# Attention with scores from one-pass halves of two heads at a time, and value products that carry the row sums

## The reference

```python
q = rmsnorm(q.reshape(B, N, 8, 64), g_q)          # 8 query heads
k = rmsnorm(k.reshape(B, N, 2, 64), g_k)          # 2 key heads, 4 query heads each
...
k_all = jnp.concatenate([kc_, kl], axis=1)        # 256 context + 512 latent keys
v_all = jnp.concatenate([vc_, vl], axis=1)
...
def gqa_attend(qb, k, v):
    s = jnp.einsum('bqhgd,bkhd->bhgqk', qb, k, preferred_element_type=jnp.float32) * HEAD_DIM ** -0.5
    p = jax.nn.softmax(s, axis=-1)
    return jnp.einsum('bhgqk,bkhd->bqhgd', p.astype(v.dtype), v)
```

## Time and profile before

| | |
|---|---|
| runs | 4133.22, 4141.39, 4142.72 us; median 4141.39 |
| the profiled execution | 4152.68 us; its span from first to last instruction 4149.8 us |
| busy share of the span | PE 87%, PEld 73%, DVE 55%, ACT 30%, POOL 28% |
| mean granted TensorE clock | 0.916 of full speed |
| attention, layer 0 | 451.95 us (first copy of keys) to 628.0 us (last unit_out) |
| attention, layer 1 | 1667.64 us to 1797.1 us |

### The profile page before, as it was taken

How to read it: one execution, slowest core, us unless ns; L and a number is a source line. 1 busy time by engine, 2 the same in 40 slices (tenths; PEclk the granted TensorE clock), 3 DMA queues, 4 the chain that set the end, 5 groups by cost and what they waited for, 6 DMA issues and landing times. The chain is left out here.

```text
span 4149.8 us, 56879 instructions
## 1 busy us (share of the span) xinstructions
PE 3610.2 (87%) x22004; PEld 3014.9 (73%) x22004; DVE 2273.7 (55%) x3284; ACT 1255.5 (30%) x1878; POOL 1162.5 (28%) x564
## 2 busy tenths in 40 slices
PE   5976797899998976889996999798999996987998
PEld 3766576788887765667885788677777775765886
DVE  4669462655546448535445588733666655326334
ACT  4123222211222123223323354432333432323222
POOL 5214002222222203024441333143222220423442
PEclk8988599899999988999998999899999997998998
DMA  4420001223222430013331211121011110212221
GB/s 164 154 93 1 0 1 61 77 97 112 97 91 93 142 105 1 1 58 115 117 111 44 77 66 71 36 102 67 32 47 37 41 47 1 102 61 72 98 95 60
DMA packets 85332, 295.30 MB, mean 71 GB/s; under 512 B 13506, under 2 KB 14082, under 8 KB 84740
## 3 DMA queue, kind: packets, MB, share of 16 engines
q1 hardware_dynamic: 84836, 290.74, 19.8%
q10 hardware_dynamic: 288, 1.60, 0.1%
HBM read 290.21 MB, written 2.10 MB: 70 GB/s over the span
## 5 line engine op out<-in xcount | busy, mean ns | idle before, releaser
L221 POOL TENSOR_TENSOR mlp_slab_lo<-slab,mlp_slab_hi 128x1024 fp32r<-128x1024 f32 x192 | 477.1, 2488 | 889.2 <-ACT mlp_slab_hi L204 889.2
L119 PE MATMUL banks<-mlp_hid_hi,mlp_slab_hi 128*128 128x512 f32 (+1 forms) x1024 | 375.0, 366 | 8.9 <-DVE mlp_hid_lo L1798 8.9
L120 PE MATMUL banks<-mlp_hid_lo,mlp_slab_hi 128*128 128x512 f32 (+1 forms) x1024 | 372.7, 364 | 0.0
L121 PE MATMUL banks<-mlp_hid_hi,mlp_slab_lo 128*128 128x512 f32 (+1 forms) x1024 | 372.4, 364 | 0.0
L204 ACT ACTIVATE mlp_slab_hi<-slab 128x1024 fp32r<-128x1024 f32 x192 | 202.4, 1058 | 528.8 <-PE banks L121 400.9
L119 PE MATMUL banks<-hT_mlp_hi,mlp_slab_hi 128*128 128x512 f32 (+1 forms) x768 | 276.6, 360 | 15.5 <-issue 8.7
L1798 DVE TENSOR_TENSOR mlp_hid_lo<-mlp_sq,mlp_hid_hi 128x512 fp32r<-128x512 f32 (+1 forms) x96 | 216.4, 2254 | 117.9 <-ACT mlp_hid_hi L1756 117.5
L120 PE MATMUL banks<-hT_mlp_lo,mlp_slab_hi 128*128 128x512 f32 (+1 forms) x768 | 275.7, 359 | 0.0
L121 PE MATMUL banks<-hT_mlp_hi,mlp_slab_lo 128*128 128x512 f32 (+1 forms) x768 | 274.9, 358 | 0.0
L119 PEld LDWEIGHTS banks<-mlp_hid_hi,mlp_slab_hi 128*128 128x128 f32 x1024 | 194.2, 190 | 43.8 <-DVE mlp_hid_lo L1798 13.8
L121 PEld LDWEIGHTS banks<-mlp_hid_hi,mlp_slab_lo 128*128 128x128 f32 x1024 | 194.0, 189 | 30.3
(11 more groups left out here) (532 smaller groups left out, 9330.4 us busy)
## 6 DMA issues: line engine op xcount, KB each, us to landing
slab<-in_s_mlp_dram SPq DMA_DIRECT2D x192, 512.0 KB, 3.5
proj_vec_slab<-in_s_vec_proj_dram SPq DMA_DIRECT2D x64, 512.0 KB, 3.7
mlp_vec_slab<-in_s_vec_mlp_dram SPq DMA_DIRECT2D x64, 512.0 KB, 3.5
slab<-in_s_ssm_dram SPq DMA_DIRECT2D x48, 512.0 KB, 3.5
slab<-in_s_gdn_dram SPq DMA_DIRECT2D x48, 512.0 KB, 3.5
slab<-in_s_in_dram SPq DMA_DIRECT2D x32, 512.0 KB, 4.6
slab<-in_s_out_dram SPq DMA_DIRECT2D x24, 512.0 KB, 4.2
slab<-in_s_merge_ssm_dram SPq DMA_DIRECT2D x24, 512.0 KB, 3.5
```

The source lines that it names most:

```text
L119: nc.tensor.matmul(out, lhs.hi, rhs.hi, start=start, stop=False)
L120: nc.tensor.matmul(out, lhs.hi, rhs.lo, start=False, stop=False)
L121: return nc.tensor.matmul(out, lhs.lo, rhs.hi, start=False, stop=stop)
L221: self.nc.gpsimd.tensor_tensor(pair.lo[:], self.raw[u % slots][:], pair.hi[:].bitcast(F32), ALU.subtract).then_inc(self.split, 1)
```

## The change

Only `attention` changes.

1. Queries and keys are split when they are prepared: ScalarE rounds each transposed tile to `hi` (queries times 1/8 already), VectorE writes `lo` (a difference). Query tiles that no unit needs (the context tiles in layer 1) are no longer prepared.
2. Scores are made for two heads at a time (units 2m and 2m+1), as three float32r products each; the matmuls of the even head use rows 0 to 63 of the array and banks 0 and 1, those of the odd head rows 64 to 127 and banks 2 and 3, in alternation. Scores of pair m wait for both exponentials of pair m-1.
3. Values are copied to `vs` with a column of ones behind each key head, so that a product has 2 x 65 = 130 columns and the row sum comes out of it. The reciprocal is taken from PSUM, in `unit_out`.
4. The row maximum is negated in the same instruction. The exponential has no scale and no accumulation.
5. ScalarE copies the first four transposed blocks, VectorE the other two.

```diff
+    prep = [(t, "keys") for t in range(C)] + [(t, "heads") for t in range(first, C)]
-        qkT = sb("qkT", [P, 6, TOK])
+        qs = sbuf_pair(st.held.enter_context, nc, f"{name}_qs", [P, HEADS_Q // 2, (C - first) * P])
+        ks = sbuf_pair(st.held.enter_context, nc, f"{name}_ks", [P, HEADS_KV, TOK])
+        vs = sb("vs", [P, C, HEADS_KV, HD + 1])
...
             def _(act):
+                for n, (t, what) in enumerate(prep):
+                    src, pair = prepared(n)
+                    act.wait_ge(turned, n + 2)
+                    nc.scalar.activation(pair.hi, src, ACT.Copy, scale=1.0 if what == "keys" else HD ** -0.5).then_inc(rounded, 1)
+                def exp(n):
+                    act.wait_ge(maxed, n + 2)
                     if n >= 2:
                         act.wait_ge(p_turned, n)
+                    nc.scalar.activation(p_[:, n % 2, 0:keys(units[n][1]) * P], scored_in(n), ACT.Exp, bias=sm[:, 0, n:n + 1]).then_inc(exped, 1)
+                def turned_out(n):
+                    act.wait_ge(p_turned, n + 2)
+                    if n >= 2:
+                        act.wait_ge(o_full, n)
+                    w = min(keys(units[n][1]), 4) * P
+                    nc.scalar.activation(pT[:, n % 2, 0:w], c.ps[:, 4 + 2 * (n % 2), 0:w], ACT.Copy).then_inc(pT_first, 1)
+                exp(0)
+                exp(1)
+                for n, (h, t) in enumerate(units):
+                    if n % 2 == 0:
+                        turned_out(n)
+                    if n + 2 < len(units):
+                        exp(n + 2)
+                    if n % 2:
+                        turned_out(n)
...
             def _(dve):
+                nc.vector.memset(vs[:, :, :, HD:], 1.0)
+                nc.vector.tensor_copy(vs[:, :, :, 0:HD], c.tok[:, :, C_AV:C_AV + P].rearrange("p t (g e) -> p t g e", g=HEADS_KV)).then_inc(v_ready, 1)
+                for n, (t, what) in enumerate(prep):
+                    src, pair = prepared(n)
+                    dve.wait_ge(rounded, n + 2)
+                    nc.vector.scalar_tensor_tensor(out=pair.lo, in0=src, scalar=1.0 if what == "keys" else HD ** -0.5,
+                                                   in1=pair.hi.bitcast(F32), op0=ALU.mult, op1=ALU.subtract).then_inc(split, 1)
+                def row_max(n):
+                    dve.wait_ge(scored, n // 2 + 2)
+                    nc.vector.tensor_reduce(sm[:, 0, n:n + 1], scored_in(n), AX, ALU.max, negate=True).then_inc(maxed, 1)
+                def unit_out(n):
+                    h, t = units[n]
+                    col = 256 + (HD + 1) * (h // 4)
+                    dve.wait_ge(o_full, n + 2)
+                    nc.vector.reciprocal(sm[:, 1, n:n + 1], c.ps[:, 5 + 2 * (n % 2), col + HD:col + HD + 1]).then_inc(inverted, 1)
+                    dve.wait_ge(inverted, n + 2)
+                    nc.vector.tensor_scalar(c.tok[:, t, C_AQ + h * HD:C_AQ + (h + 1) * HD], c.ps[:, 5 + 2 * (n % 2), col:col + HD],
+                                            sm[:, 1, n:n + 1], None, ALU.mult).then_inc(o_read, 1)
+                def turned_rest(n):
...
+                for n in range(0, len(units), 2):
+                    if n + 2 < len(units):
+                        row_max(n + 2)
+                        row_max(n + 3)
+                    turned_rest(n)
+                    if n:
+                        unit_out(n - 1)
+                    turned_rest(n + 1)
+                    unit_out(n)
...
             def _(pe):
+                def scores(m):
+                    h, t = units[2 * m]
+                    if m:
+                        pe.wait_ge(exped, 2 * m + 1)
+                    q = qs[:, h // 2, (t - first) * P:(t - first + 1) * P]
+                    k = ks[:, h // 4, :]
+                    spans = ((0, HALF), (HALF, TOK)) if keys(t) == TILES else ((0, CTX),)
+                    for b, (s0, s1) in enumerate(spans):
+                        for e, (x, y) in enumerate(((q.hi, k.hi), (q.lo, k.hi), (q.hi, k.lo))):
+                            for n in range(2):
+                                r = slice(64 * n, 64 * n + 64)
+                                last = nc.tensor.matmul(c.ps[:, 2 * n + b, 0:s1 - s0], x[r], y[r, s0:s1], start=e == 0, stop=e == 2)
+                    last.then_inc(scored, 1)
                 def weighted(n):
+                    pe.wait_ge(pT_first, n + 2)
+                    if keys(t) > 4:
+                        pe.wait_ge(pT_rest, wide_before(n) + 2)
                     for s in range(keys(t)):
+                        last = nc.tensor.matmul(c.ps[:, 5 + 2 * (n % 2), 256:256 + HEADS_KV * (HD + 1)], pT[:, n % 2, s * P:(s + 1) * P],
+                                                vs[:, s, :, :].rearrange("p g e -> p (g e)"), start=s == 0, stop=s == keys(t) - 1)
...
                 for n, (h, t) in enumerate(units):
-                    if n + 1 < len(units):
-                        scores(n + 1)
+                    if n % 2 == 0 and n + 2 < len(units):
+                        scores(n // 2 + 1)
                     pe.wait_ge(exped, n + 2)
                     if n >= 2:
                         pe.wait_ge(o_read, n)
```

More of the change, by code:

```diff
@@ L1361, in _ @@
-                unit_out(dve, len(units) - 1)
+                last.then_inc(k_ready, 1)
+                nc.vector.memset(vs[:, :, :, HD:], 1.0)
[5 more added lines that the diff above has]
+                                                   in1=pair.hi.bitcast(F32), op0=ALU.mult, op1=ALU.subtract).then_inc(split, 1)
@@ new lines, in turned_rest @@
+                def turned_rest(n):
+                    nk = keys(units[n][1])
+                    if nk > 4:
+                        dve.wait_ge(p_turned, n + 2)
+                        if n >= 2:
+                            dve.wait_ge(o_full, n)
+                        nc.vector.tensor_copy(pT[:, n % 2, HALF:nk * P], c.ps[:, 5 + 2 * (n % 2), 0:nk * P - HALF]).then_inc(pT_rest, 1)
+                row_max(0)
+                row_max(1)
+                for n in range(0, len(units), 2):
[7 more added lines that the diff above has]
+                    unit_out(n)
@@ L1363, in _ @@
+                unit_out(len(units) - 1)
             @block.tensor
             def _(pe):
-                pe.wait_ge(qk_ready, 2)
-                n = 0
-                for t in range(C):
-                    src = [c.tok[:, t, C_AQ + P * j:C_AQ + P * j + P] for j in range(4)] + \
-                          [kdup[:, t, 2 * j:2 * j + 2, :].rearrange("p d e -> p (d e)") for j in range(2)]
-                    for half in range(2):
-                        if n >= 8:
-                            pe.wait_ge(placed, n - 6)
-                        for j in range(3):
-                            last = nc.tensor.transpose(c.ps[:, n % 8, j * P:(j + 1) * P], src[3 * half + j], c.ident)
-                        last.then_inc(turned, 1)
-                        n += 1
@@ L1377, in _ @@
-                pe.wait_ge(placed, 2 * C + 1)
-                def scores(n):
-                    h, t = units[n]
-                    r = slice(64 * (h % 2), 64 * (h % 2) + 64)
-                    if n >= 2:
-                        pe.wait_ge(exped, n)
-                    q = qkT[r, h // 2, t * P:(t + 1) * P]
-                    for b, (s0, s1) in enumerate(((0, HALF), (HALF, TOK)) if keys(t) == TILES else ((0, CTX),)):
-                        last = nc.tensor.matmul(c.ps[:, 2 * (n % 2) + b, 0:s1 - s0], q, qkT[r, 4 + h // 4, s0:s1], start=True, stop=True)
+                pe.wait_ge(k_ready, 2)
@@ new lines, in _ @@
+                for n, (t, what) in enumerate(prep):
+                    if n >= 8:
+                        pe.wait_ge(split, n - 6)
+                    for j in range(HEADS_KV if what == "keys" else 4):
+                        src = kdup[:, t, 2 * j:2 * j + 2, :].rearrange("p d e -> p (d e)") if what == "keys" else c.tok[:, t, C_AQ + P * j:C_AQ + P * j + P]
+                        last = nc.tensor.transpose(c.ps[:, n % 8, j * P:(j + 1) * P], src, c.ident)
+                    last.then_inc(turned, 1)
```

61 lines of the change are left out of this document (16 added, 45 removed).

## The result

| | before | changed | |
|---|---|---|---|
| median of the runs compared | 4141.2 us (4 runs) | 4087.3 us (4 runs, 4085.6 to 4096.4) | ratio 0.9875, 95% interval 0.9857 to 0.9894 |
| profiled execution | 4152.7 us | 4085.6 us | -67.1 |
| attention stages, first key copy to last output, both layers | 305.5 us | 259.0 us | -46.5 |
| from layer 0's last output to layer 1's first key copy | 1039.6 us | 1023.5 us | -16.1 |

The kernel became faster, by 54 us of the median where 35 were forecast. 4087.3 lies just under the range given (4090 to 4126). The last line of the table is a surprise: the code of that stretch is the same in both kernels.

What follows compares the result with a forecast made beforehand. TensorE was taken to set attention's pace. Wide pairs -28.8, narrow pairs -5.0, clock -5, start and end +5 and preparation -1 summed to -35 us: profiled execution 4118, median 4106 us, range 4090 to 4126.

Steps and rivals of the forecast that it cites:

- What bounds: Attention stretches of both layers: TensorE goes on without a wait and sets the pace, 3.63 us per wide unit.
- Wide pairs: Two heads' units with six key tiles at 2.4 GHz: 6.36 us against 7.26; 32 pairs give -28.8 us.
- hand-off: Transposes wait for VectorE to read the previous output from PSUM: 0.79 us once a pair.
- The overlap of row halves: Paired scores: both heads' products run side by side, 1.03 us for the pair plus 0.20.
- rival (c): Scores: row halves take turns, wide pairs 7.39 us, total 4150, no change; chance 0.06.
- The 1.48 us of one unit's scores: Wide unit before: four passes (1.28) plus 0.20 for changing between 64 and 128 rows and emptying the array.
- Narrow pairs: Layer 0 units with two key tiles, at 1.2 GHz: 4.62 us against 5.24; eight pairs give -5.0 us.
- the clock rises after about one pair: Layer 0's wide part: full clock after about one pair, -5 us (ends 0 and -7).
- start and end: Attention's beginning 1.6 us longer, its end about 0.9: +5 us for two layers.
- rival (a): Clock rises already among the narrow pairs, 3.0 to 3.3 us each, 11 us less: 4095; chance 0.18.
- Rival (d): Clock stays at 1.2 GHz because TensorE stands still in each pair: +115, 4256 us; chance 0.05.
- Start, end, preparation: Attention's edges +5 us for two layers; preparation 0 in layer 0, -1 us in layer 1.

Runs made afterwards that it cites:

- in turn: Changed kernel with only the score order altered: within each key span, the even head's three products, then the odd head's; 4099.0 us.
- on all rows: Changed kernel with four-pass, unpaired scores, each product using 128 rows instead of 64 (output not the reference's); 4093.6 us.
- one pass unpaired: Changed kernel with its one-pass score products, but scores made unit by unit in the order of the kernel before; 4094.6 us.
- the two runs with added transposes: Layer 0's preparing transposes repeated: 96 more TensorE instructions in the changed kernel, 4105.4 us; 174 more in the kernel before, 4117.4 us (0.9941).

## Why the prediction was right and wrong

**What bounds.** Right: attention was 46.5 us of the gain in the profiled executions, and TensorE sets its pace in both kernels.

**Wide pairs.** 32 x 0.99 = 31.7 us against 28.8. Scores 1.26 (1.23), hand-off 0.67 (0.79), transposes and products as forecast. The overlap of row halves, read off one row of layer 1's start, was right, and rival (c) is out: even in turn the halves ran side by side. The 1.48 us of one unit's scores was read rightly too: on all rows it is 1.30, so 0.19 goes to the change of rows.

**Narrow pairs and the clock: the step that failed first.** "Narrow pairs, at 1.2 GHz: ... Eight pairs: -5.0 us" and "I take it that the clock rises after about one pair: -5 us", meant for the wide part, should have been one term. The clock was back after 13.7 us, among the narrow pairs, and stayed up but for 3.4 us. I had held it back to the wide part, with "TensorE stands idle some 0.8 of each pair" against an earlier rise. With start and end (+5 forecast; layer 1 lost 1.1) these three terms were to give -5. They gave -15.8: -10.3 from layer 0's first score to its sixteenth output, -6.6 in its wide part beyond the 16 pairs, +1.1 in layer 1. That is rival (a), priced at 11 us and given 0.18; its narrow pair (3.0 to 3.3) measured 3.14. Its reason, that the scores now fill all rows, is not shown. The run on all rows agrees with it, but it is one execution, and one pass unpaired, on 64 rows, had the clock back just as early. So the rise in the narrow part is measured and its cause stays open. Rival (d) did not come: the clock was at 1.00 from 494.2 us on. The rule by which transposes don't count as busy (the Trainium skill, TensorE: Matmul & The Clock Gate, Part 4) is contradicted once more: 11.6 us of transposes alone kept the clock at 1.00.

**Start, end, preparation.** +1.0 in layer 0 (0 forecast) and -0.1 in layer 1 (-1). Sum of attention: -31.7 - 15.8 + 0.9 = -46.6, measured -46.5.

**The term that was missing.** "the next stage starts behind a barrier, so a microsecond saved in attention is one saved at the end" took the rest of the program for constant. The change also lengthened TensorE's code by 193 instructions in layer 0's attention, and so moved a later loop to where its jumps do not have to wait for their code: 16.1 us, and 13 to 14 in the two runs with added transposes. With 96 instructions more, which brought the waits back, the changed kernel took 4105.4 us, inside the range and within 1 us of the 4106 forecast, though not for the same reasons: attention gave more than forecast. By these numbers the clock's 11 us and these 13 to 16 put the time under 4090 together; either alone would have left it above. This second part is luck: nothing in the change aims at where the MLP's code lies. The trace of before had the sign of it, two waits of L119 for "issue" with loads on the instruction queue beside them; the Trainium skill states the mechanism (Runtime: NRT & Kernel Launch, Instruction fetch mechanics: a taken branch whose target is not held waits for a fetch), and the traces agree: TensorE waited 3.5 to 5.2 us a time over the five profiles that have it.

**What does not add up.** 46.5 and 16.1 us are more than the 53.9 between medians. The profiled execution of before was 11 us over its median, and 4.3 of the 67.1 us between the two profiled executions lie ahead of attention, in code that is the same (first key copy at 452.0 and 447.7 us). Executions of the kernel before spread over 4113.2 to 4149.9 in 43 single times, with one between 4127 and 4133. For 39 of them the mean granted clock is known too, and it parts them: the nine under 4127 have 0.922 to 0.925, the other thirty 0.916 to 0.921. The two means differ by 0.0052, which over 4140 us is some 43 us at 0.50 and 21 us of time (an estimate from these numbers). That is about what the kernel before gained where its clock did not fall in the narrow units (attention 17.1 us shorter). None of the nine was profiled, so it is not shown that they are executions in which attention kept its clock. If they are, part of the gain in the narrow part is one that the kernel before has too, in about one execution of four.

## What to carry to other kernels

Put a wait where the contested bank is first touched, not ahead of the group that touches it: that one line was worth 26 us here, half of what the whole change brought. Where TensorE is full and yet at 1.2 GHz, as on 64 rows here for over 50 us, look at how the stretch is entered: with a denser preparation, attention took 17 us less in the kernel before. Whether the rows in use matter beside it was not separated. And when an edit changes the number of instructions ahead of a loop, look at the loop's own time before crediting the edit.

## What the runs showed of the hardware that was not expected

- Products for the two row halves ran side by side even where the program has three of one half and then three of the other; a half's first product started 0.01 us after the other's first.
- One kind of work has two lasting states of the clock: the narrow units of the kernel before ran at 0.50 for 43 us, and at 1.00 throughout where the clock had not fallen at their start.
- A loop's jump back cost a wait of 3.5 to 5.2 us and 6.8 us of lower clock, or nothing, by the number of instructions ahead of it: with 1784, 1817 or 2073 in layer 0's attention in all five profiles, with 1945 to 1977 in none of fourteen.
